# Operand splits and memory squares moved between engines in a two-layer hybrid decoder trunk (RWKV-7, then dilated attention)

## The reference, cut to what matters

```python
h = rmsnorm(x, attn_norm[0])
p = h @ a_w_in                                     # r, k, v, wd, ad, gd, q_mem
xs = p + (prev - p) * mu                           # prev: the row before
w_log = -softplus(-(w0 + tanh(wd) @ w2)) - 0.5     # decay
a = sigmoid(a0 + ad @ a2)                          # rate
g = sigmoid(gd) @ g2                               # gate
...                                                # the recurrence over 512 tokens
y = (layernorm(ys) * lnx_w + lnx_b + bonus) * g    # bonus = sum(r * k * r_k) * v
kv = rmsnorm(mem, mem_norm) @ mem_w_kv             # 256 memory tokens
```

## Time and profile before

| | |
|---|---|
| median of 3 runs | 1325.53 us (1324.45 to 1325.69) |
| the profiled execution | 1325.26 us |
| its span in the profile | 1323.5 us |
| mean granted TensorE clock | 0.999 of 2.4 GHz |
| TensorE busy | 1290.4 us, 97%, 10448 matmul records |
| VectorE busy | 807.3 us, 61% |
| ScalarE busy | 590.8 us, 45% |
| GpSimd busy | 375.8 us, 28% |

### The profile page before, as it was taken

The page is one execution under the profiler, slowest core; times in us unless marked ns, Lnnn a source line. Parts: engine busy times, 40 slices in busy tenths (PEclk is TensorE's granted clock), DMA queues, the critical chain, the costliest instruction groups (busy, mean ns, idle before and its releaser), DMA issues.

```text
span 1323.5 us, 25887 instructions
## 1 busy us (share of the span) xinstructions
PE 1290.4 (97%) x10448; PEld 1025.4 (77%) x10448; DVE 807.3 (61%) x1142; ACT 590.8 (45%) x940; POOL 375.8 (28%) x342
## 2 busy tenths in 40 slices
PE   7999999999999999999999999998999999999999
PEld 5876777776578888888888888776778888888887
DVE  4777777776457666256664448548576662466642
ACT  6575645563244443134444445547554441244421
POOL 4369777774321110001111145330211100011100
PEclk9999999999999999999999999999999999999999
DMA  8100111114023333223332242110123332233331
GB/s 322 49 25 28 55 54 39 54 36 163 18 96 95 95 107 109 85 80 95 98 123 82 92 143 81 62 51 31 41 88 98 101 122 92 79 96 95 119 112 40
DMA packets 30045, 114.22 MB, mean 86 GB/s; under 512 B 3456, under 2 KB 5248, under 8 KB 29184
## 3 DMA queue, kind: packets, MB, share of 16 engines
q1 hardware_dynamic: 29952, 112.89, 26.2%
HBM read 110.78 MB, written 2.10 MB: 85 GB/s over the span
## 4 chain that ended last, share of the span: by engine, by line
PE 85%; DVE 5%; ACT 3%; issue 2%; POOL 0%; DVEq 0%; ACTq 0%
PE bank L577 84%; PE bank L1247 1%; DVE arena L1921 1%; ACT arena L1444 0%; DVE sin_part L2291 0%; DVE cos_part L2318 0%; DVE in_lo L1932 0%; PE bank L1131 0%; DVE head_stat L2301 0%; ACT w_hi L1327 0%; PE bank L1154 0%; DVE x L2199 0%; DVE stat L1999 0%; DVE cos_part L2287 0%; DVE arena L2012 0%
## 5 line engine op out<-in xcount | busy, mean ns | idle before, releaser
L1327 ACT ACTIVATE w_hi<-ring 128x1024 fp32r<-128x1024 f32 (+1 forms) x144 | 162.3, 1127 | 261.8 <-PE bank L577 261.8
L577 PE MATMUL bank<-in_hi,w_hi 128*128 128x512 f32 x704 | 274.9, 390 | 0.9 <-DVE in_lo L1932 0.9
L577 PE MATMUL bank<-in_hi,w_lo 128*128 128x512 f32 x704 | 273.9, 389 | 0.0
L577 PE MATMUL bank<-in_lo,w_hi 128*128 128x512 f32 x704 | 273.9, 389 | 0.0
L1907 DVE TENSOR_TENSOR w_lo<-ring,w_hi 128x1024 fp32r<-128x1024 f32 (+1 forms) x124 | 165.2, 1332 | 65.2 <-ACT w_hi L1327 64.9
L2623 POOL TENSOR_TENSOR z_raw<-silu,conv 128x512 f32<-128x512 f32 x40 | 51.6, 1289 | 537.8 <-DVE conv L2242 503.4
L577 PEld LDWEIGHTS bank<-in_hi,w_hi 128*128 128x128 f32 x704 | 132.2, 188 | 29.4 <-DVE in_lo L1932 1.3
L577 PEld LDWEIGHTS bank<-in_lo,w_hi 128*128 128x128 f32 x704 | 132.2, 188 | 27.8 <-issue 0.5
L577 PEld LDWEIGHTS bank<-in_hi,w_lo 128*128 128x128 f32 x704 | 132.2, 188 | 27.6
L577 PEld LDWEIGHTS bank<-arena 64*64 64x64 f32 (+2 forms) x4064 | 110.0, 137 | 48.6 <-issue 40.5
L2242 DVE SCALAR_TENSOR_TENSOR conv<-up_raw,par,conv 128x511 f32<-128x511 f32 (+1 forms) x176 | 131.8, 749 | 17.4 <-DVE conv L2242 9.8
(11 more groups left out here) (278 smaller groups left out, 2157.6 us busy)
## 6 DMA issues: line engine op xcount, KB each, us to landing
ring<-w_ring SPq DMA_DIRECT2D x119, 512.0 KB, 3.5
ring<-w_ring SPq DMA_DIRECT2D x32, 704.0 KB, 4.1
ring<-w_pairs SPq DMA_DIRECT2D x18, 512.0 KB, 3.8
arena<-w_mem SPq DMA_DIRECT2D x2, 2048.0 KB, 19.4
arena<-w_ring SPq DMA_DIRECT2D x4, 512.0 KB, 4.9
x<-xT SPq DMA_DIRECT2D x1, 2048.0 KB, 7.8
outT<-x SPq DMA_DIRECT2D x8, 256.0 KB, 2.0
mask<-masks SPq DMA_DIRECT2D x1, 1536.0 KB, 7.8
```

Source lines behind the costliest of these rows:

```text
L577: return nc.tensor.matmul(out, lhsT, rhs, start=first, stop=last, skip_group_check=True)
L1327: return nc.scalar.activation(out, in_, ACT.Copy)
```

## The change

Three things are done.

1. **Memory squares.** VectorE adds the eight slices of squares in place (seven additions of 128x256 in `memh[0][:, 0, :]`, counted on `x_acc` behind the seven for x), and TensorE makes one product with the ones in place of eight. TensorE now waits there for all fourteen additions.
2. **Splits of the gate and low-rank inputs.** `sig_hi`, the new `lora_hi`, and `blk_r` are copied by ScalarE within the memory attention ahead of step 0; `sig_lo` and the new `lora_lo` are made by VectorE in step 0 behind the maximum of the third block of scores. The low parts lie where the operands themselves lay.
3. **Decay and rate products of pairs 1 to 5** are six fp32r products in place of two fp32 ones, the two halves in turn. For this ScalarE copies `ws_hi` behind `rrk_hi`, and VectorE makes `ws_lo` behind `rrk_lo`, in steps 0 to 4 (`bonus_low`); in step 0 both subtractions now stand behind the fourth Gram eviction and ahead of `Btok`. TensorE waits for `ws_lo` in place of the transfer of `ws`.

```diff
--- before.py
+++ after.py
@@ -172,11 +172,16 @@
             h_hi = tensor(rwkv_layer, "h_hi", [P, KD, T], F32R)
             q_hi = tensor(rwkv_layer, "q_hi", [P, OSLOTS, QW], F32R)
             q_lo = tensor(rwkv_layer, "q_lo", [P, OSLOTS, QW], F32R)
+            with ExitStack() as lows:
+                lora_lo = tensor(lows, "lora_lo", [P, T], F32R)[:, :]
+                sig_lo = tensor(lows, "sig_lo", [P, T], F32R)[:, :]
+                ws_lo = tensor(lows, "ws_lo", [P, P], F32R)[:, :]
+                wg_lo = tensor(lows, "wg_lo", [P, P], F32R)[:, :]
             arena = tensor(rwkv_layer, "arena", [P, ARENA])
+            lora_hi = tensor(rwkv_layer, "lora_hi", [P, T], F32R)[:, :]
             sig_hi = tensor(rwkv_layer, "sig_hi", [P, T], F32R)[:, :]
-            sig_lo = tensor(rwkv_layer, "sig_lo", [P, T], F32R)[:, :]
+            ws_hi = tensor(rwkv_layer, "ws_hi", [P, P], F32R)[:, :]
             wg_hi = tensor(rwkv_layer, "wg_hi", [P, P], F32R)[:, :]
-            wg_lo = tensor(rwkv_layer, "wg_lo", [P, P], F32R)[:, :]
             rrk_hi = tensor(rwkv_layer, "rrk_hi", [P, T], F32R)[:, :]
             rrk_lo = tensor(rwkv_layer, "rrk_lo", [P, T], F32R)[:, :]
             blk_r = tensor(rwkv_layer, "blk_r", [P, P], F32R)[:, :]
@@ -399,6 +404,18 @@
         def krv_bank(t, back):
             return (2, 3, 6 if back else 2)[t]
 
+        def gate_parts(j):
+
+            return 3 * j + (2 if j <= PAIRS - 1 else 1)
+
+        def bonus_parts(j):
+
+            return 3 * j + 3
+
+        def rank_parts(j):
+
+            return 3 * j + 4
+
         def decay_bank(back):
             return 3 if back else 0
 
@@ -629,11 +646,8 @@
                 quartered_tile(bank[i][:, :], N_QM0 + i)
             quartered_tile(bank[4][:, :], N_LORA)
             pe.wait_ge(sem("tables_in"), 32)
-            for k in range(KD):
-                pe.wait_ge(sem("msq"), k + 1)
-                q = mm(bank[6][:, 0:NMEM], ones, memh[0][:, k, :], k == 0, k == KD - 1)
-            q.then_inc(sem("mem_ss"), 1)
-            pe.wait_ge(sem("x_acc"), KD - 1)
+            pe.wait_ge(sem("x_acc"), 2 * (KD - 1))
+            mm(bank[6][:, 0:NMEM], ones, memh[0][:, 0, :]).then_inc(sem("mem_ss"), 1)
             for c in range(RES):
                 mm(bank[3][:, 2 * c:2 * c + 2], acc[:, c * P:(c + 1) * P], ones[:, 0:2])
             mm(bank[7][:, :], ones, acc).then_inc(sem("x_ss"), 1)
@@ -890,9 +904,19 @@
 
             def lora_products(j, back):
 
-                pe.wait_ge(sem("ws_in"), 16 * j + 16)
+                out = [bank[b(back)][:, :] for b in (decay_bank, lora_bank)]
+                if j == 0:
+                    pe.wait_ge(sem("ws_in"), 16)
+                    for i in range(2):
+                        mm(out[i], ws[head(i), :], lora[head(i), :]).then_inc(sem("lora_mm"), 1)
+                    return
+                pe.wait_ge(sem("part_lo"), rank_parts(j - 1))
                 for i in range(2):
-                    mm(bank[(decay_bank, lora_bank)[i](back)][:, :], ws[head(i), :], lora[head(i), :]).then_inc(sem("lora_mm"), 1)
+                    mm(out[i], ws_hi[head(i), :], lora_hi[head(i), :], True, False)
+                for i in range(2):
+                    mm(out[i], ws_hi[head(i), :], lora_lo[head(i), :], False, False)
+                for i in range(2):
+                    mm(out[i], ws_lo[head(i), :], lora_hi[head(i), :], False, True).then_inc(sem("lora_mm"), 1)
 
             def step(j, front, back, post, fill):
 
@@ -927,7 +951,7 @@
                     if v == 1 and post:
                         y_to_features(j)
                     if v == 2 and back:
-                        pe.wait_ge(sem("part_lo"), 2 * j + 1)
+                        pe.wait_ge(sem("part_lo"), gate_parts(j))
                         if post:
                             pe.wait_ge(sem("y_ln"), j - 1)
                         mm(bank[6][:, :], wg_hi, sig_hi, True, False)
@@ -1466,6 +1490,11 @@
             for i in range(2):
                 mem_exps(0, i)
                 memory_value(1, i)
+                if i == 0:
+                    act.wait_ge(sem("lora_in"), 3)
+                    copy(sig_hi, sig_g).then_inc(sem("part_hi"), 1)
+                    copy(lora_hi, lora).then_inc(sem("part_hi"), 1)
+                    copy(blk_r, blk)
 
             def bchunks(a):
                 return a.rearrange("p (c t) -> p c t", t=CHUNK)
@@ -1586,8 +1615,6 @@
                     own_part(vx, krv_bank(2, back), j, MUV, "own")
                     if not back:
                         mem_output(0, 3)
-                        copy(sig_hi, sig_g).then_inc(sem("part_hi"), 1)
-                        copy(blk_r, blk)
                 if back:
                     for i in range(2):
                         act.wait_ge(sem("pq_mm"), 2 * j + (i - 1))
@@ -1597,6 +1624,10 @@
                 if front:
                     act.wait_ge(sem("rk"), j + 1)
                     copy(rrk_hi, rrk).then_inc(sem("part_hi"), 1)
+                    if j < PAIRS - 1:
+                        act.wait_ge(sem("ws_in"), 16 * j + 32)
+                        act.wait_ge(sem("lora_mm"), 2 * j + 2)
+                        copy(ws_hi, ws).then_inc(sem("part_hi"), 1)
                 if back:
                     state(j, 1)
                     state(j, 2)
@@ -1944,6 +1975,10 @@
                 if k > 1:
                     dve.wait_ge(sem("x_acc"), k - 1)
                 V.tensor_tensor(acc, x_sq[0] if k == 1 else acc, x_sq[k], ALU.add).then_inc(sem("x_acc"), 1)
+            for k in range(1, KD):
+                dve.wait_ge(sem("msq"), k + 1)
+                dve.wait_ge(sem("x_acc"), KD - 2 + k)
+                V.tensor_tensor(memh[0][:, 0, :], memh[0][:, 0, :], memh[0][:, k, :], ALU.add).then_inc(sem("x_acc"), 1)
             def token_eps(b, e, n):
 
                 dve.wait_ge(sem("x_ss"), e)
@@ -2071,6 +2106,10 @@
                         .then_inc(sem("cc"), 1)
                     if not back:
                         mem_bound(0, 2)
+                        dve.wait_ge(sem("part_hi"), 2)
+                        lower(sig_lo, sig_g, sig_hi, "part_lo")
+                        dve.wait_ge(sem("lora_mm"), 2)
+                        lower(lora_lo, lora, lora_hi, "part_lo")
                 if post:
                     dve.wait_ge(sem("y_sq"), j - 1)
                     V.tensor_reduce(ysd, ysq, AX.X, ALU.add).then_inc(sem("y_sum"), 1)
@@ -2102,7 +2141,7 @@
                     V.tensor_tensor(y[:, bass.ds(j - 2, 1), :], yln.unsqueeze(1), gate.unsqueeze(1), ALU.mult)\
                         .then_inc(sem("y_out"), 1)
                 if back:
-                    dve.wait_ge(sem("part_hi"), 2 * j + 1)
+                    dve.wait_ge(sem("part_hi"), gate_parts(j))
                     lower(wg_lo, wg, wg_hi, "part_lo")
                     inverse_add(j, 2)
                 if front:
@@ -2143,11 +2182,8 @@
                 if front:
                     dve.wait_ge(sem("own"), 3 * j + 5)
                     shifted(vx, bank[krv_bank(2, back)], pcol(j, MUV), "shifted")
-                    if not back:
-                        dve.wait_ge(sem("part_hi"), 1)
-                        lower(sig_lo, sig_g, sig_hi, "part_lo")
-                    dve.wait_ge(sem("part_hi"), 2 * j + 2)
-                    lower(rrk_lo, rrk, rrk_hi, "part_lo")
+                    if back:
+                        bonus_low(j)
                 if back:
                     dve.wait_ge(sem("rp_mm"), j)
                     V.tensor_tensor(MT.rearrange("p (c w) d -> p w c d", w=2),
@@ -2170,10 +2206,20 @@
                             dve.wait_ge(sem("gr_mm"), 2 * j + (half + 1))
                             V.tensor_tensor(flat2(Gm[:, hh, 2 * half:2 * half + 2, :, :]), bank[2 + hh][:, :],
                                             flat2(tri_d[:, hh, 2 * half:2 * half + 2, :, :]), ALU.mult).then_inc(sem("gr_ev"), 1)
+                    if not back:
+                        bonus_low(j)
                     dve.wait_ge(sem("tok_mm"), 4 * j + 4)
                     V.tensor_tensor(Btok.rearrange("p c h d -> p h c d"), turned_tokens(0),
                                     d2.rearrange("p c h -> p h c").unsqueeze(3).to_broadcast([P, 2, CP, HD]), ALU.mult)\
                         .then_inc(sem("b_tok"), 1)
+
+            def bonus_low(j):
+
+                dve.wait_ge(sem("part_hi"), bonus_parts(j))
+                lower(rrk_lo, rrk, rrk_hi, "part_lo")
+                if j < PAIRS - 1:
+                    dve.wait_ge(sem("part_hi"), rank_parts(j))
+                    lower(ws_lo, ws, ws_hi, "part_lo")
 
             dve.wait_ge(sem("zeroed"), 1)
             step(0, True, False, False)
```

## The result

The changed kernel took **1329.31 us** (median of 10 runs, 1327.15 to 1331.45), the kernel before in the same series 1325.61 (1324.45 to 1326.03): ratio 1.0025, 95% interval 1.0017 to 1.0033. It is 3.7 us slower where I forecast 2.2 us faster, and outside my range.

A forecast was written before the change was run, and what follows sets the result against it. TensorE, 85% of the chain, was taken to bound the kernel, with its idle before 345 us deciding. Terms -2.8 + 1.2 - 0.9 + 0.3 = -2.2 us gave 1323.1 profiled, 1323.3 us as median forecast; range 1321.0 to 1326.2.

The forecast's parts named there:

- Memory squares: Opening: seven of TensorE's eight products go, 3.02 us, less 0.2 for collision with GpSimd: -2.8 us.
- my bound: Opening: VectorE's seven adds end between 26.8 and 28.1 us, before TensorE wants the sum at 29.64.
- Gate and rank splits: Ahead of and in step 0: ScalarE's and VectorE's splits hidden in waits of 3.88 and 3.89 us, cost 0.
- End of step 0: `rrk_lo`, GpSimd's mask operation and `ws_lo` come ahead of the rank products, starting at 114.7 against 113.51: +1.2 us.
- Rank products: Five pairs as three overlapping fp32r rounds, 0.88 us each against 1.06: -0.9 us in all.
- `ws_lo` in steps 1 to 4: VectorE's `ws_lo` behind `rrk_lo` delays L2153 by 0.15 us in steps 2 and 3; others have room: +0.3 us.
- below 0.7: Sign expected in the profile after: each `ws_lo` of steps 1 to 4 takes below 0.7 us.
- The sum: All terms together: -2.8 + 1.2 - 0.9 + 0.3 = -2.2 us, from 1325.26 to 1323.1 us for the profiled execution.
- From there TensorE runs 30.58 us without a break: Behind the start of step 0's rank products at 113.51 us, TensorE was read as running 30.58 us without idle.
- my rivals: End of step 0 smooth, 1322.0 us (chance 0.32); opening gains nothing, 1326.1 (0.13); 64-row fp32r at fp32 rate, 1332.8 (0.06).
- three signs of being wrong: Reciprocal moves under 2.5 us; a rank pair takes over 1.1 us; step 0's rank products start outside 110.7 to 113.1.

The follow-up runs named there:

- rank_early: Changed kernel with step 0's `ws_lo` made ahead of the Gram evictions and `rrk_lo` behind `Btok`: 1325.30 us; with 16 idle instructions 1322.08 us.
- before_pad56: Kernel before, nothing changed but 56 idle instructions ahead of TensorE's first product: 1329.65 us, ratio 1.0027.
- pad16: Changed kernel with 16 idle instructions ahead of TensorE's first product: 1325.19 us.
- rank_back: Changed kernel with the rank products of all pairs fp32 again; memory sum and sig splits stay changed: 1326.88 us; with 28 idle instructions 1321.90 us.
- opening_back: Changed kernel with the eight memory-sum products on TensorE again and VectorE's seven adds taken out: 1329.10 us.

## Why the prediction was wrong

Term by term, against the profiled execution after:
- *Memory squares, -2.8.* -2.62 at the reciprocal. Right; the adds ended at 29.16, a microsecond after my bound, still ahead of 30.04.
- *Gate and rank splits, 0.* Right: the waits of 3.9 us that cover them are still 2.6 us on both engines.
- *End of step 0, +1.2.* The rank products start at 112.13, where I had 111.9; `ws_lo` took 1.35 us. Against the opening's -2.62 that is +1.24. Right, by the mechanism named: GpSimd goes in between. rank_early shows that it was avoidable.
- *Rank products, 0.88 a pair.* 0.89 in step 0 and 0.89 in step 1 (152.49 to 153.38). Right in length. Whether the four later pairs pass their 0.17 us on is not to be seen under the gaps.
- *`ws_lo` in steps 1 to 4, +0.3.* 0.70 us each, on the edge of my "below 0.7". No new wait for it or for what stands behind it shows in the waits above.
- **The sum had no term for what moves when nothing is added to a path.** "From there TensorE runs 30.58 us without a break" was as far as I looked into the steps; the earlier trace rows showed 8.5 us of idle in the stretch behind, and I took all of it as fixed. 6.6 us of it was "issue", all but 0.9 at boundaries in TensorE's program. The change moved every one of them by 8 to 24 instructions against the work. Between the two gate products the idle grew by 5.7 us, from 7.0 to 12.6, and the 3.4 us at the lower clock, which the kernel before had there and the one after had not, took 1.4 off again: 4.3 us lost in place of 0.4 gained. That is 4.7 of the 5.3 us by which the profiled execution missed the 1323.1 of the sum (the median missed by 6.0). This is the step that failed, "from there TensorE runs without a break" and the idle behind it taken as fixed, and none of my rivals had it; none of the three signs of being wrong that I had named showed, since all three look at the changed parts themselves. I counted the instructions for what they take, and not for where they leave the ones behind them.

Is the loss the clock's instead? The nine other executions after were granted 0.997 or 0.998 on average, the profiled one 1.000, and so part of the median's 0.9 us above it may be the clock's. But the profiled execution, at the full clock, is still 3.1 us slower than the profiled one before, and before_pad56 is 4.1 slower with seven of its nine executions at 0.999 or above.

That the kernel before stood at good places shows in before_pad56 (+4.1 us). At equal or nearly equal places the changed kernel is level with it or a little faster (1325.19 against 1325.88), and it would be clearly faster with `ws_lo` made earlier.

Between the two gate products idle and clock together account for the differences. The gaps called issue are 3.8 us in the 198.98 of pad16, 5.1 in 199.27 of before, 11.4 in 203.57 of after, 10.3 in 204.69 of rank_back. With all idle taken out, TensorE's busy time between them is 190.2 to 191.2 us in the four profiled executions that have no stretch at the lower clock there, 192.1 to 193.0 in the nine with one of 3.4 us, and 193.9 in the one with 6.8 us. Each such stretch of any run, up to the last of the steps, began within, or less than 2 us behind, an idle of TensorE of 1.8 to 2.8 us; but the changed kernel has a wait and a gap of 2.0 us without one.

Left open: when a packet of instructions starts, and so how long one boundary waits, and which gap is followed by the lower clock. Openings with the same code differed by up to 1 us between executions.

## What to carry to other kernels

When a change adds or drops instructions on an engine that runs short instructions back to back, look for idle labelled "issue" in the middle of runs of like records, and count the records between two of them: a constant count is the supply of the program, not the work, and the packets of the instruction queue, which end just ahead of such gaps, confirm it. Then compare versions at equal places in the program, or with a few idle instructions put where the engine waits anyway, before a part is kept or dropped. Otherwise a gain of 4 us reads as a loss of 1, as that of rank_back did (1321.90 at the places of the kernel before, 1326.88 without idle instructions).

## What I had not expected of the hardware

- Ahead of the first product, 16 waits that are already met took 4.1 us off the changed kernel; 56 put 4.1 us onto the kernel before. A gap at a boundary lasted from 0.2 to 2.8 us.
- Within quiet stretches one boundary follows the other by about 4 us once both show a gap (146.03 to 150.15, 268.46 to 272.33; the shortest of any run is 3.6), where the records between, without the gap, take 2.8. The packets break this up: from 146.03 it is 1.6 us until the packet starts, 1.2 until it ends, 1.3 until the next product.
- In most of the profiled executions TensorE's clock fell to 0.50 for 3.4 or 6.8 us in or behind a long gap, which cost some 1 to 2 us for each 3.4 (opening_back: 1.5).
- The Trainium skill (Advanced Engine Details and Errata, section ISA Cache) gives 128 KB on TensorE and "Only 2 cache lines!" of 256 instructions. The packets here agree with few blocks ahead, not with the eight of 128 KB: at each of the 111 gaps TensorE waits for a packet that starts only after the boundary before.
- A met wait costs TensorE 0.11 us (240 of them, 27.1 us).
- `ws_lo`, 128x128, costs 0.40 us alone and 1.35 next to GpSimd's operation.
